# A decoder block in fp32 on one core: the one-hot matrices of the second token tile are built in another way

## The reference

```python
q = (x @ wq).reshape(b, s, PEER_HEADS, 2, PEER_DQ // 2)
sc = jnp.einsum('bshcd,hckd->bshck', q, subkeys)
top_s, top_i = lax.top_k(sc, PEER_TOPK)
...
best_s, best_j = lax.top_k(cand.reshape(b, s, PEER_HEADS, 256), PEER_TOPK)
expert = ...                      # i * 128 + j, i and j in 0..127
g = jax.nn.softmax(best_s, axis=-1)
...
act = jax.nn.gelu(jnp.einsum('td,tkd->tk', xc, u[ec]))
return jnp.einsum('tk,tkd->td', gc * act, v[ec])
```

## Time and profile before

| | us |
|---|---|
| runs | 1906.73, 1904.01, 1903.4; median 1904.01 |
| the profiled execution, its own time | 1902.88 |
| its span in the profile | 1900.8 |
| mean granted TensorE clock | 0.839 of full speed |

### The profile page before, as it was taken

One profiled execution on the slowest core, in us unless ns is written; L12 is line 12 of the kernel. 1 busy time (PEld: TensorE's weight loads), 2 busy tenths in 40 slices (PEclk: granted clock), 3 DMA queues, 4 the chain that ended last, 5 costly groups with the idle time before them and its releaser, 6 DMA issues.

```text
span 1900.8 us, 25603 instructions
## 1 busy us (share of the span) xinstructions
PE 1333.4 (70%) x8243; PEld 1196.9 (63%) x8243; DVE 1447.6 (76%) x2032; ACT 761.9 (40%) x1350; POOL 810.6 (43%) x898
## 2 busy tenths in 40 slices
PE   5999999989995553000111122269999999999997
PEld 5999999989984441000111111267888888888897
DVE  4334555564368878999999999898999989999854
ACT  3333445554210012100555666654343343334544
POOL 2100000000054434555555555288777777777303
PEclk8999999999997776555555555599999999999999
DMA  8874444356489999999999999908999999999952
GB/s 261 260 237 134 135 142 140 119 174 199 151 328 411 411 415 399 378 409 399 409 411 411 407 415 402 404 0 311 365 364 369 362 366 363 364 362 369 321 185 104
DMA packets 184264, 578.25 MB, mean 304 GB/s; under 512 B 14628, under 2 KB 113269, under 8 KB 149888
## 3 DMA queue, kind: packets, MB, share of 16 engines
q0 software_dynamic: 58544, 367.16, 49.0%
q1 hardware_dynamic: 125648, 210.14, 32.3%
HBM read 573.03 MB, written 7.36 MB: 305 GB/s over the span
## 4 chain that ended last, share of the span: by engine, by line
PE 56%; DVE 20%; DMA 11%; issue 7%; ACT 3%; POOL 1%; DVEq 0%; SPq 0%; ACTq 0%; POOLq 0%
PE banks L1974 15%; DVE rows L1433 15%; PE banks L1685 15%; PE banks L1982 8%; DMA wqraw<-peer_wq_dram 7%; PE banks L1642 6%; PE banks L1892 3%; PE banks L1960 3%; DMA rows<-peer_u_dram,expert 2%; ACT whi L762 1%; POOL hot L715 1%; DMA pproj<-ple_proj_dram 1%; DVE wlo L1271 1%; PE banks L1912 1%; PE banks L1714 1%
## 5 line engine op out<-in xcount | busy, mean ns | idle before, releaser
L1433 DVE SCALAR_TENSOR_TENSOR rows<-rows,banks 128x2048 f32<-128x2048 f32 x232 | 520.1, 2279 | 29.5 <-DMA rows<-peer_u_dram,expert 28.9
L648 POOL DMA_INDIRECT rows<-peer_u_dram,expert x232 | 220.5, 950 | 267.3 <-DVE rows L1433 173.4
L694 POOL DMA_INDIRECT vrow<-peer_v_dram,vidx x224 | 280.0, 1250 | 114.1 <-DVE hres L1508 64.6
L1938 PE MATMUL banks<-hot,hot 128*128 128x128 f32 x512 | 101.7, 368 | 251.8 <-ACT hot L1036 233.1
L1938 PEld LDWEIGHTS banks<-hot,hot 128*128 128x128 f32 x512 | 89.5, 267 | 264.3 <-issue 178.2
L1508 DVE SCALAR_TENSOR_TENSOR hres<-vrow,slot_coef,hres 128x704 f32<-128x704 f32 x224 | 213.0, 951 | 2.3 <-DMA vrow<-peer_v_dram,vidx 2.1
L762 ACT CAST whi<-raw 128x2048 fp32r<-128x2048 f32 x80 | 152.0, 1901 | 147.7 <-PE banks L1685 106.7
L1982 PE MATMUL banks<-vlo,chi 128*128 128x192 f32 x762 | 192.2, 388 | 0.0
L1203 DVE TENSOR_TENSOR wlo<-raw,whi 128x2048 fp32r<-128x2048 f32 x47 | 108.3, 2305 | 101.2 <-ACT whi L762 100.0
L1522 DVE TENSOR_TENSOR vlo<-vraw,vhi 128x1216 fp32r<-128x1216 f32 x128 | 181.2, 1415 | 0.0
L599 POOL CAST bidxf<-bidx 128x32 f32<-128x32 uint32 x16 | 3.5, 217 | 415.8 <-DVE bidx L1397 415.8
(11 more groups left out here) (267 smaller groups left out, 3158.5 us busy)
## 6 DMA issues: line engine op xcount, KB each, us to landing
vraw<-peer_v_dram SPq DMA_DIRECT2D x128, 672.0 KB
raw<-w_in_dram SPq DMA_DIRECT2D x48, 1024.0 KB, 5.7
raw<-w_out_dram SPq DMA_DIRECT2D x16, 1024.0 KB, 5.7
wqraw<-peer_wq_dram SPq DMA_DIRECT2D x32, 512.0 KB, 7.4
raw<-ple_gate_dram SPq DMA_DIRECT2D x16, 1024.0 KB, 5.8
hres<-x_dram SPq DMA_DIRECT2D x4, 1024.0 KB, 5.9
rows<-peer_u_dram,expert POOLq DMA_INDIRECT x232
vrow<-peer_v_dram,vidx POOLq DMA_INDIRECT x224
```

What stands on the lines that cost most here:

```text
L648: pool.indirect_dma_start(dst[:, :], None, peer_u[0], bass.IndirectOffsetOnAxis(ap=expert[b][:, k:k + 1], axis=0))\
L694: pool.indirect_dma_start(vrow[j][:, :], None, pieces, bass.IndirectOffsetOnAxis(ap=idx[:, j % TT, j // TT:j // TT + 1], axis=0))\
L1433: dve.scalar_tensor_tensor(out=r[:, :], in0=r[:, :], scalar=1.0, in1=xps[tt][:, :], op0=ALU.mult, op1=ALU.mult, accum_out=dots[b][:, k:k + ...
L1938: last = pe.matmul(bank[SPREAD_BANK[m]][:, a * P:(a + 1) * P], hot2[tt][m][:, a, :], hot1[tt][m][:, a, :], start=True, stop=True)
```

## The change

The two sets of tile 1 are divided otherwise. VectorE now compares without a weight, for all groups and both sets, four tokens in one instruction of 512 elements. It reads the numbers 0 to 127 from PSUM (`iotap`, in bank 2) and not from SBUF; a copy puts them there once the last row product of tile 1 has read the bank. GpSimd no longer builds one-hots: it multiplies `hot2` in place by the weights, one instruction of 512 elements per group. TensorE waits for both VectorE instructions and for the multiplication of its group. The copy of four indices (`idx4`) and its semaphores are gone.

```diff
+    iotap = bank[2][:, 0:NKEYS]
...
-            def even_first_hots(i, m, peeled):
-                n = 2 * i + m // 2
-                if not peeled:
-                    pool.wait_ge(spread_mm[1], 4 * i + m - 3)
-                if not (peeled and m == 0):
-                    pool.wait_ge(hot1_ready, TOKB * n)
-                pool.tensor_copy(idx4[:, :], tsl[1][:, 0, bass.ds((4 * i + m) * TOKB, TOKB)]).then_inc(idx4_ready, 1)
-                pool.wait_ge(idx4_ready, n + 1)
+            def weigh_hots(i, m):
+                q = 4 * i + m
+                pool.wait_ge(hot2_ready, 2 * q + 1)
                 pool.nop(nofuse=True)
-                for a in range(TOKB):
-                    pool.tensor_scalar(hot1[1][m][:, a, :], iota[:, :], idx4[:, a:a + 1], None,
-                                       ALU.is_equal).then_inc(hot1_ready, 1)
+                pool.tensor_tensor(hot2[1][m][:, :, :], hot2[1][m][:, :, :],
+                                   tsl[1][:, 2, bass.ds(TOKB * q, TOKB)][:, :, None].broadcast_to([P, TOKB, NKEYS]),
+                                   ALU.mult).then_inc(weighted, 1)
             pool.wait_ge(tsl_sb[1], 1)
-            for m in (0, 2):
-                even_first_hots(0, m, True)
+            for m in range(4):
+                weigh_hots(0, m)
...
                 if not peeled:
                     dve.wait_ge(spread_mm[1], q - 3)
-                if m % 2:
-                    dve.tensor_tensor(hot1[1][m][:, :, :], iota[:, None, :].broadcast_to([P, TOKB, NKEYS]),
-                                      tsl[1][:, 0, bass.ds(TOKB * q, TOKB)][:, :, None]
+                for c, hot in ((1, hot2[1][m]), (0, hot1[1][m])):
+                    dve.tensor_tensor(hot[:, :, :], iotap[:, None, :].broadcast_to([P, TOKB, NKEYS]),
+                                      tsl[1][:, c, bass.ds(TOKB * q, TOKB)][:, :, None]
                                       .broadcast_to([P, TOKB, NKEYS]), ALU.is_equal).then_inc(hot2_ready, 1)
-                for a in range(TOKB):
-                    t = TOKB * q + a
-                    dve.tensor_scalar(hot2[1][m][:, a, :], iota[:, :], tsl[1][:, 1, bass.ds(t, 1)],
-                                      tsl[1][:, 2, bass.ds(t, 1)], ALU.is_equal, ALU.mult).then_inc(hot2_ready, 1)
...
+            dve.wait_ge(eaten, PEER_STEPS * TOPK)
+            dve.tensor_copy(iotap[:, :], iota[:, :]).then_inc(iota_copied, 1)
+            dve.wait_ge(iota_copied, 1)
             dve.wait_ge(tsl_sb[1], 1)
...
-                    pair = 2 * i + m // 2
-                    if m % 2 == 0:
-                        pe.wait_ge(hot1_ready, TOKB * (pair + 1))
-                    pe.wait_ge(hot2_ready, (2 * TOKB + 1) * pair + (TOKB, 2 * TOKB + 1)[m % 2])
+                    pe.wait_ge(hot2_ready, 2 * q + 2)
+                    pe.wait_ge(weighted, q + 1)
```

More of the change, by code:

```diff
@@ L303, in build @@
     ssqs = place("ssqs", [P, TT, D // CHUNK_C])
-    idx4 = place("idx4", [P, TOKB])
     vidx = [place(f"vidx{r}", [P, TT, VBODY // 2], i32) for r in range(2)]
@@ L362, in build @@
     tsl_mm, tsl_sb = [[sem(f"{n}{t}") for t in range(TT)] for n in ("slots_transposed", "slots_copied")]
+    iota_copied = sem("iota_in_psum")
     hot_dist, hot_unit = sem("hot_distances"), sem("hot_units")
-    hot_ready, hot1_ready = sem("tile0_one_hots"), sem("tile1_even_first_one_hots")
-    hot2_ready, idx4_ready = sem("tile1_one_hots"), sem("indices_of_four_tokens")
+    hot_ready, weighted = sem("tile0_one_hots"), sem("tile1_weighted_one_hots")
+    hot2_ready = sem("tile1_one_hots")
     spread_mm, spread_sb = [[sem(f"{n}{t}") for t in range(TT)] for n in ("spread_products", "spread_copied")]
@@ L688, in v_fetch @@
                     if first and j in FIRST_OVER_HOTS:
-                        pool.wait_ge(hot2_ready, (2 * TOKB + 1) * SPREADS // 2)
+                        pool.wait_ge(hot2_ready, 2 * SPREADS)
                         pool.wait_ge(spread_sb[1], SPREADS)
@@ L700, in _ @@
             pool.wait_ge(eaten, PEER_STEPS * TOPK)
-            def even_first_hots(i, m, peeled):
-                n = 2 * i + m // 2
-                if not peeled:
-                    pool.wait_ge(spread_mm[1], 4 * i + m - 3)
-                if not (peeled and m == 0):
-                    pool.wait_ge(hot1_ready, TOKB * n)
-                pool.tensor_copy(idx4[:, :], tsl[1][:, 0, bass.ds((4 * i + m) * TOKB, TOKB)]).then_inc(idx4_ready, 1)
-                pool.wait_ge(idx4_ready, n + 1)
+            def weigh_hots(i, m):
+                q = 4 * i + m
+                pool.wait_ge(hot2_ready, 2 * q + 1)
                 pool.nop(nofuse=True)
-                for a in range(TOKB):
-                    pool.tensor_scalar(hot1[1][m][:, a, :], iota[:, :], idx4[:, a:a + 1], None,
-                                       ALU.is_equal).then_inc(hot1_ready, 1)
+                pool.tensor_tensor(hot2[1][m][:, :, :], hot2[1][m][:, :, :],
+                                   tsl[1][:, 2, bass.ds(TOKB * q, TOKB)][:, :, None].broadcast_to([P, TOKB, NKEYS]),
+                                   ALU.mult).then_inc(weighted, 1)
             pool.wait_ge(tsl_sb[1], 1)
-            for m in (0, 2):
-                even_first_hots(0, m, True)
+            for m in range(4):
+                weigh_hots(0, m)
             with pool.Fori(1, SPREADS // 4) as i:
-                for m in (0, 2):
-                    even_first_hots(i, m, False)
+                for m in range(4):
+                    weigh_hots(i, m)
             v_index(0, 0)
```

## The result

The median of four runs is 1890.83 us (1890.0 to 1891.45), the ratio to the kernel before 0.9925 with a 95% interval of 0.9912 to 0.9939. Measured twice more beside the experiments, the changed kernel came to 0.9932 (0.9917 to 0.9948) and 0.9932 (0.9915 to 0.9949), a gain of 13. So the miss of the range is small and hangs on how the ratio is formed; the miss of the gain, 13 to 14 for 10.3, does not.

The account below looks back on a forecast made before the run. Tile 1's one-hot stage was bound by GpSimd and VectorE together, 3.09 us per two groups. Shortening it by 10.3 took the profiled 1902.88 to 1892.6; the median lies 1.13 higher, so 1893.7 us, range 1890.5 to 1898.5.

Parts of the forecast that it names:

- the stage's gain goes through one to one: Tile 1's one-hot stage, before the dense products: whatever it loses shortens the kernel equally; 10.3 us forecast.
- the 1 us either way: Start of the dense products: TensorE's clock may dip for a different time than before, 1 us more or less.
- the 1.28 us of GpSimd's multiplication: Per group in the stage: one multiplication of 512 elements taken as 1.28 us, lower bound 1.06, upper 1.45.
- who paces: Per group in the stage: GpSimd narrowly, 1.28 us, against VectorE 1.22, TensorE 1.03, ScalarE 0.97.
- VectorE paces: Rival in the stage: with a 1.06 multiplication VectorE's 1.22 sets the pace, 1892, chance 0.15; dearer VectorE, 1896 to 1897.5, 0.10.
- my sum: Whole stage: 32 multiplications of 1.28 plus beginning and end, last copy at 1278.5 instead of 1288.8, 10.3 us shorter.
- the operand in PSUM: VectorE's comparisons in the stage: reading the numbers from PSUM adds nothing to 0.68 us; the skill's page implied 0.13 per group.
- the two engines don't shut each other out: Stage: VectorE and GpSimd run side by side; the opposing rival had 2.50 us per group, 1935, chance 0.05.
- sequencer work: VectorE in the stage: 0.18 us counted as hidden behind long instructions; otherwise 1.22 per group becomes 1.31 to 1.40.
- the ring of four: Stage's four buffers: a round of some 3.6 us fits into 4 x 1.28 = 5.1, so they do not bind.
- the late `vlo`: After the stage: first `v` row's wait grows 0.9 us, delaying the first `vlo`, covered by 2.3 us of slack.
- the six: Stage's beginning: TensorE's clock is full some 6 us after it began, as before, until about 1242.4.

Follow-up runs that it names:

- Run 4: Changed kernel with GpSimd multiplying each token's matrix by one row of 128 numbers, not one number per token: ratio 0.9940 to the kernel before, stage 43.44 us.
- run 2: Changed kernel with VectorE reading the numbers from SBUF and GpSimd copying one number per group instead of multiplying: 1890.32 us (one run), stage 41.75 us.
- run 5: Changed kernel, numbers still in PSUM, with GpSimd copying one number per group instead of multiplying: ratio 0.9932 to the kernel before, stage 41.48 us.
- run 3: Kernel before, its division of work kept, with VectorE reading the numbers from PSUM in both kinds of comparison: ratio 0.9984, stage 53.44 us.
- Run 1: Changed kernel with VectorE's comparisons reading the numbers from SBUF, so both inputs lie there: ratio 1.0069 to the kernel before, stage 69.47 us.

## Why the prediction was right or wrong

**Right: that the stage's gain goes through one to one.** The dense products have nothing to wait for but this stage. From TensorE's first product to the transposition at the end of the dense part are 493.9 us before and 494.1 after. In another execution of the changed kernel, the third, it is 495.2: there the granted clock averages 0.52 from 1280 to 1286 us, where it is 0.81 in the first. This is the 1 us either way that the prediction allowed.

**Wrong, and the step that failed: the 1.28 us of GpSimd's multiplication, and with it who paces.** It lasts 1.040, below the lower bound of 1.06. Between two rows, 1285 and 1057 ns, I chose the one that is overwritten in place. Run 4 shows what divides them: the second input. With a row along the elements 1.268, with one number repeated 1.040. The cheap row was the like of the new instruction, since it too repeats one number along the innermost elements; overwriting in place costs nothing that shows (1.040 in place, 1.057 not). With 1.04 GpSimd has 0.16 to spare, and the rival "VectorE paces", to which I gave 0.15, is what happened. Its 1892 lies 1 to 2 us above the measured time.

**Mis-sized besides: a duration was taken for a spacing.** Run 4 has the multiplication that I took mine for, 1.268 long. Its pace is 1.23, and its stage 43.4 us where my sum says 55.1 - 10.3 = 44.8. So of the 2.8 us by which the stage's gain was under-forecast, 1.4 are the form of the operand, and 1.4 lie between my sum and run 4: some 1.1 the spacing, 31 x (1.268 - 1.232), the rest mostly that 1.28 was a little long. For VectorE I did use the spacing, 0.61; it was 0.598.

**Right: the operand in PSUM.** 681 ns, as the row of an instruction with one input there said, and not 65 ns more. The sentence of the Trainium skill ("Perfetto Trace Analysis", Optimizing Scalar/DVE Operations, more overhead on PSUM) is not borne out at 512 elements (run 2 from SBUF and run 5 from PSUM have the same spacing, 0.60). At 128 run 3 has 421 ns against 335, which goes its way; but those are TENSOR_SCALARs and the others TENSOR_TENSORs, and no run shows whether the size or the kind makes the difference. The 2.5 us that I worked out from that page were also a little high: a pace of 1.35 in place of 1.28 makes 32 x 0.07 = 2.2.

**Right: that the two engines don't shut each other out, and why.** Run 1 shows the price where they do, 2.05 us per group; the prediction's 2.50 was too high. It also read the earlier trace rows a little wrong: the VectorE instruction there does not end with GpSimd's (22.95) but 0.55 later (19.49 + 4.01 = 23.50), and run 1 has the same 0.55. The row it rested on, one GpSimd instruction beside VectorE's two kinds, was worth more than the warning of the Trainium skill ("Perfetto Trace Analysis", Optimizing Scalar/DVE Operations) that offloading between those two might not help. The warning is true of run 1 and false of the change.

**Right in the small:** the copy to PSUM is hidden (the wait for `tsl` is still 1.37); sequencer work does not show; the ring of four is long enough; the first `v` row waits 1.29, "some 1.2"; TensorE does not wait for the late `vlo`, with 1.3 us to spare. TensorE begins 2.1 us after the first comparison, 2.3 forecast. The granted clock averages 0.59 from 1238 to 1242 us, between its two levels of 0.50 (1.2 GHz) and 1.00 (2.4 GHz), and is 1.00 behind that. So it rose within some four us of TensorE's first product, in the two other executions of the changed kernel too, where it took six before; I had copied the six. Why it rose sooner is not shown.

**The range.** Its lower end was the forecast less 3.2, with VectorE's pace taken as 1.22. It missed the first measurement, read as a ratio, by 0.8 us; the two later ones, at 1891.1, lie in it. The open cost had a lower bound taken from one row of another shape, and I let the range go hardly below it.

## What to carry to other kernels

When work is divided between VectorE and GpSimd, look at where VectorE's inputs lie before counting instructions: beside GpSimd's multiplication the same two instructions took 1.20 us per group with one of VectorE's inputs in PSUM and 2.05 with both in SBUF; without it they took 1.20 from SBUF too. Judge the parts of such a change together: one was worth 1.7 us, the other minus 14.3, both 13.1. For a GpSimd instruction that the trace lacks, take the row whose inputs repeat in the same way, and where engines work back to back count from start to start, not by duration.

## What the runs showed of the hardware that was not expected

- GpSimd's TENSOR_TENSOR of 128x512 lasts 1.040 us when the second input repeats one number along the row, 1.268 when it runs along it.
- VectorE's comparison of 128 numbers (a TENSOR_SCALAR) lasts 335 ns from SBUF and 421 from PSUM (run 3); that of 512 numbers (a TENSOR_TENSOR) 678 in the kernel before and 681 in the changed one, 700 in run 3. From start to start the small ones are 0.255 apart from SBUF, (1.10 - 0.335) / 3, and 0.32 from PSUM, so four of them lose some 0.26 us to PSUM; the long ones stay 0.60 apart and lose nothing.
- A GpSimd copy of a single number takes 0.44 us beside a VectorE instruction with two SBUF inputs, 0.18 beside one with one of them in PSUM.
